# Four feed-forwards split into an up stage and a down stage, the down stage computed with seven block products

## The chip, the cores and the metric

The kernel runs on one core of one Trainium2 chip, in float32 throughout. The metric is device time in microseconds (us), the median over several executions. Engines are named as the profile names them: PE (TensorE, matmul), PEld (its weight load, which overlaps PE), DVE (VectorE), ACT (ScalarE), POOL (GpSimd) and SP (SyncE, which here issues the transfers of the weights).

## The reference, cut to what matters

A first block (modulated norm, hybrid mixer, mixture of experts) is followed by two layers of a second block. Each of these layers runs a feed-forward, a mixer, a cross attention and a feed-forward, so there are four feed-forwards. The sequence has 256 tokens, the model width is 1024, and the hidden width `D_FF` is 2816.

```python
def swiglu_ffn(h, w_in, w_out):
    gate, up = jnp.split(h @ w_in, 2, axis=-1)
    return (jax.nn.silu(gate) * up) @ w_out

for l in range(DEPTH_2):
    x = x + FFN_RES_WEIGHT * swiglu_ffn(rms_norm(x, ffn1_norm_g[l]), ffn1_w_in[l], ffn1_w_out[l])
    ...   # mixer: x + concat(rwkv, moba) @ w_mix_out
    ...   # x + memory_cross_attention(...)
    x = x + FFN_RES_WEIGHT * swiglu_ffn(rms_norm(x, ffn2_norm_g[l]), ffn2_w_in[l], ffn2_w_out[l])
return rms_norm(x, final_norm_g)
```

## The kernel before, in words

**Tiling.** The hidden width is cut into 11 groups `g` of 256 columns (`NGRP`, `FB`). The tokens are two tiles of 128. A matmul takes a stationary tile of 128x128 and a moving tile of up to 512 columns; one call of `nc.tensor.matmul` in float32 is two MATMUL instructions in the trace, each with its own LDWEIGHTS.

**Up-projection of a group** (`up`, PE rows of L2029). Gate and linear columns of one group are a product of (2 halves of K) by (2 halves of tokens) by (gate, linear). Group 0 is done plainly (`up_first`, L2007, 16 products of 128x512). Groups 1 to 10 use the form of Strassen's scheme with seven products P1 to P7, each over four tiles of K with 256 moving columns: 28 matmuls, 56 instructions. It needs sums of the tokens (`Sx`, four, made once for a feed-forward at L2725 to L2730) and sums of the weights (`Tw`, four per group at 128x1024, L2746, L2752, L2756, L2762; two buffers, by `g % 2`). The products go through three PSUM banks, 0 to 2. ACT copies P1 and P5 to SBUF (L2500), DVE adds up the four results (L2771) in `hidden`, ACT takes the silu of the gate (L2503), DVE multiplies gate and linear into `hh` (L2793).

**Turning.** PE transposes `hh` (four tiles, L2015) into bank 3, ACT copies it to `fh` (128x512, two buffers by `g % 2`).

**Down-projection of a group** (`down`, PE rows of L2064). Two tiles of K, two token tiles and two halves of 512 output columns are 8 matmuls of 128x512, 16 instructions. They accumulate over all 11 groups in four banks, 4 to 7, one per token tile and half. The turning of the next group is put in the middle of it.

**Order.** PE runs up(1), down(0), up(2), down(1), then a loop of four turns with up(3), down(2), up(4), down(3), and at last down(10). DVE and ACT run loops of the same kind, and SP issues the pieces of weights in that order: two transfers of 1 MB for an up piece, one of 1 MB for a down piece, in a ring of four slots of 2 MB (`SLOTS`, `ring`). A slot is loaded again once PE has finished with what was in it (semaphores `hid_up` and `hid_down`). The pieces of the mixer and the cross attention follow in the same ring.

**End of a feed-forward.** When the four banks of the down-projection are complete, DVE scales and adds them into `x` (L2824, four instructions of 128x512: two after the first half of the columns, which releases `x_first`, two after the second, which releases `x_ready`). PE then transposes `x` for what follows (L302, `raw_transposes`): banks 0 and 1 wait for `x_first`, banks 2 and 3 for `x_ready`. After the last feed-forward comes the final norm (ACT row sums, POOL, DVE L3099) and the store.

**Beside it.** In the first feed-forward of each layer POOL multiplies the memory by its gain (`gm`, L1959), once `xT` is complete.

## Time and profile before

| what | us |
|---|---|
| median of 3 runs | 2463.85 (2461.95 to 2465.54) |
| the profiled execution, its own time | 2462.07 |
| its span (first to last instruction) | 2460.3 |
| PE busy | 2360.7 (96% of the span) |
| PE, down-projections of the four feed-forwards (L2064) | 315.3 |
| PE, up-projections of groups 1 to 10 (L2029, all five groups of rows) | 214.4 + 144.7 + 75.6 + 75.6 = 510.3 and one smaller |
| DVE busy | 880.2 (36%) |
| DMA, mean | 203 GB/s |

The four feed-forwards stand at about 857 to 1073, 1438 to 1653, 1655 to 1870 and 2233 to 2448 us of the span. The granted TensorE clock has a mean of 0.983 over the span. Busy times of PE are unions of modelled spans: the mean of one instruction (592 ns) is longer than the distance from one start to the next, since matmuls are pipelined, so costs are read from starts.

### The profile page before, as it was taken

How to read it: one execution, taken by the hardware profiler on the slowest of the kernel's cores; microseconds unless marked ns; L12 is line 12 of the kernel's file. 1: busy time of each engine (PE TensorE's matmuls, PEld its weight loads, DVE VectorE, ACT ScalarE, POOL GpSimd, SP SyncE). 2: the span in 40 equal slices, each digit the busy share in tenths (PEclk: the TensorE clock that was granted, in tenths of full speed). 3: DMA queues.
4: the chain of work that ended last, by engine and by line, in shares of the span. 5: the costliest groups of instructions: out<-in, count | busy, mean ns of one | idle time of the engine just before them, and what ended most of it. 6: DMA issues, size and time to landing. Idle time of an engine off the chain costs nothing. (4 is left out here: it accounts for less than half of the span.)

```text
span 2460.3 us, 29787 instructions
## 1 busy us (share of the span) xinstructions
PE 2360.7 (96%) x12188; PEld 1587.7 (65%) x12188; DVE 880.2 (36%) x1620; ACT 424.2 (17%) x832; POOL 47.1 (2%) x75
## 2 busy tenths in 40 slices
PE   7999979999999899999999999999999999999998
PEld 4778744444444377778666757767777867676775
DVE  2888221111111344421542134444442154213443
ACT  1123121111111111111312211111111121221111
POOL 1000000000000000000000000000000000000000
PEclk9999979999999999999999999999999999999999
DMA  9565639999999844452431254454545243124442
GB/s 397 221 257 226 258 102 344 422 422 422 422 422 422 324 138 156 151 194 80 154 121 41 97 163 154 153 171 137 172 135 212 68 147 121 67 71 162 154 163 76
DMA packets 176139, 499.48 MB, mean 203 GB/s; under 512 B 7193, under 2 KB 99625, under 8 KB 146097
## 3 DMA queue, kind: packets, MB, share of 16 engines
q1 hardware_dynamic: 172224, 481.23, 52.3%
q0 software_dynamic: 3680, 16.43, 2.3%
q8 instruction: 68, 1.11, 0.2%
q10 hardware_dynamic: 144, 0.52, 0.1%
q14 instruction: 23, 0.18, 0.0%
HBM read 491.34 MB, written 6.82 MB: 202 GB/s over the span
## 5 line engine op out<-in xcount | busy, mean ns | idle before, releaser
L2064 PE MATMUL bank<-ring,fh 128*128 128x512 f32 x704 | 315.3, 592 | 0.0
L2064 PEld LDWEIGHTS bank<-ring,fh 128*128 128x128 f32 x704 | 130.6, 190 | 132.2 <-issue 130.1
L2029 PE MATMUL bank<-Tw,Sx 128*128 128x256 f32 x960 | 214.4, 379 | 0.0
L2029 PEld LDWEIGHTS bank<-Tw,Sx 128*128 128x128 f32 x960 | 182.1, 190 | 24.6
L2098 PE MATMUL bank<-xT,ring 128*128 128x256 f32 x704 | 152.6, 379 | 0.0
L844 PE MATMUL bank<-xT,ring 128*128 128x256 f32 x640 | 143.7, 384 | 2.8 <-ACT xT L279 2.8
L2098 PEld LDWEIGHTS bank<-xT,ring 128*128 128x128 f32 x704 | 133.4, 190 | 18.0
L2029 PE MATMUL bank<-ring,xT 128*128 128x256 f32 x640 | 144.7, 379 | 0.0
L2029 PEld LDWEIGHTS bank<-ring,xT 128*128 128x128 f32 x640 | 121.6, 190 | 33.6 <-issue 19.1
L2771 DVE TENSOR_TENSOR whole<-bank,part 128x256 f32<-128x256 f32 x120 | 51.0, 425 | 255.6 <-PE bank L2029 255.6
L844 PEld LDWEIGHTS bank<-xT,ring 128*128 128x128 f32 x640 | 122.8, 193 | 21.9 <-ACT xT L279 2.9
L1379 PE MATMUL bank<-ring,xg 128*64 128x512 f32 x512 | 114.3, 594 | 7.1 <-DMA ring<-in_w 7.1
L1416 PE MATMUL bank<-ring,hTg 128*64 128x512 f32 x512 | 113.4, 595 | 0.0
L1379 PE MATMUL bank<-more,xg 128*64 128x512 f32 x512 | 112.6, 592 | 0.0
L2500 ACT ACTIVATE part<-bank 128x256 f32<-128x256 f32 x80 | 30.7, 384 | 346.5 <-PE bank L2029 346.5
L1379 PEld LDWEIGHTS bank<-ring,xg 128*64 128x64 f32 x512 | 36.2, 137 | 82.5 <-issue 68.0
L1696 DVE TENSOR_TENSOR sg<-sg,bank 128x512 f32<-128x512 f32 x16 | 11.0, 688 | 214.0 <-PE bank L1379 214.0
L1416 PEld LDWEIGHTS bank<-ring,hTg 128*64 128x64 f32 x512 | 35.3, 137 | 76.1 <-issue 76.1
L1379 PEld LDWEIGHTS bank<-more,xg 128*64 128x64 f32 x512 | 36.7, 137 | 73.3 <-issue 73.3
L1363 PEld LDWEIGHTS bank<-hot,xs 128*128 128x128 f32 x544 | 64.9, 199 | 17.2 <-issue 13.0
L2029 PE MATMUL bank<-ring,Sx 128*128 128x256 f32 x320 | 75.6, 379 | 0.0
L2029 PE MATMUL bank<-Tw,xT 128*128 128x256 f32 x320 | 75.6, 379 | 0.0
(458 smaller groups left out, 3063.9 us busy)
## 6 DMA issues: line engine op xcount, KB each, us to landing
ring<-in_w SPq DMA_DIRECT2D x128, 1024.0 KB, 18.6
ring<-in_ffn_w_in SPq DMA_DIRECT2D x88, 1024.0 KB, 7.5
ring<-in_first_pieces SPq DMA_DIRECT2D x33, 2048.0 KB, 12.3
more<-in_w SPq DMA_DIRECT2D x64, 1024.0 KB, 19.8
ring<-in_ffn_w_out SPq DMA_DIRECT2D x44, 1024.0 KB, 4.9
ring<-in_w_mix_in SPq DMA_DIRECT2D x12, 2048.0 KB, 9.3
ring<-in_xattn_w_kv SPq DMA_DIRECT2D x8, 2048.0 KB, 11.9
ring<-in_w_mix_out SPq DMA_DIRECT2D x4, 2048.0 KB, 9.7
```

Source lines behind the costliest of these rows:

```text
L844: last = nc.tensor.matmul(b[:, c * SEQ:(c + 1) * SEQ], w[:, k, m * P:(m + 1) * P], xT[:, k, :], start=(k == 0), stop=(k == KD - 1))
L1363: last = nc.tensor.matmul(bank[half][:, k * P:(k + 1) * P], xs[:, t, f:f + P], hot[:, t, :], start=(t == 0), stop=(t == NT - 1))
L1379: last = nc.tensor.matmul(bank[2 + m][e * CAP:(e + 1) * CAP, :], xg[:, 4 * half + k, e * CAP:(e + 1) * CAP], up_rows(4 * m + 2 * half + e) ...
L1416: last = nc.tensor.matmul(bank[half][e * CAP:(e + 1) * CAP, :], hTg[:, c * P + e * CAP:c * P + (e + 1) * CAP], down_rows(8 + 2 * (c // 2) ...
L1696: nc.vector.tensor_tensor(sg[:, 1, :], sg[:, 0, :], bank[3][:, :], ALU.mult).then_inc(h_ready, 1)
L2029: last = nc.tensor.matmul(bank[b][:, 0:SEQ], lhs(k), rhs(k), start=(k == 0), stop=(k == 3))
L2064: last = nc.tensor.matmul(bank[4 + 2 * half + t][:, :], fh[:, g % 2, c * SEQ + t * P:c * SEQ + (t + 1) * P], w[:, c, half * 512:(half + 1) ...
L2098: last = nc.tensor.matmul(b[:, c * SEQ:(c + 1) * SEQ], w[:, k, col:col + P], xT[:, k, :], start=(k == 0), stop=(k == KD - 1))
L2500: nc.scalar.activation(dst, src, ACT.Copy).then_inc(ffn_copied, 1)
L2771: return nc.vector.tensor_tensor(dst, a_, b_, ALU.add)
```

## The change

All up-projections of a feed-forward run first, groups 0 to 10, and the gated rows of all groups stay in SBUF, turned (`fh` has eleven buffers in place of two). Then come the down-projections. In them the two K tiles of a group, the two token tiles and the two halves of the output columns form a two by two by two block product, done as seven matmuls of 128x512 per group. They accumulate over the groups in seven PSUM banks (`BANK_OF`), and the results are combined once at the end. For this DVE makes, per group, four sums of the gated rows (128x128: `Sd0` for group 0, else in `Sx`, four buffers) and four sums of the down weights (128x512, `Td`, four buffers laid over `Tw`).

The up-projections use seven banks in place of three, so most waits between products are gone from `up`, and DVE spreads the four weight sums of the next group between its other work. The loops of PE, DVE, ACT and SP over the groups are written out. Down weights come as six pieces of up to 2 MB (two groups each) in place of eleven of 1 MB; the numbering of the pieces in the ring changes with it. At the end, ACT copies P1 and P5 of the down stage, and DVE needs eleven instructions of 128x512 in place of four: four sums, and seven scaled additions into `x`.

```diff
         ffn = ExitStack()
-        fh = sb("fh", [2, 512], ffn)
+        fh = sb("fh", [NGRP, 512], ffn)
         hh = sb("hh", [NT, SEQ], ffn)
         fs = sb("fs", [NT, SEQ], ffn)
+        Sd0 = sb("Sd0", [4, P], ffn)
+        sb("behind_cross", [1040], ffn)
+
+        Tw = sb("Tw", [2, 4, 4, SEQ], ffn)
+        Td = [Tw[:, 1 - b // 2].rearrange("p a k n -> p (a k n)")[:, (b % 2) * 2048:(b % 2 + 1) * 2048].rearrange(
+            "p (a n) -> p a n", a=4) for b in range(4)]
         gf2_row = sb("gf2_row", [D], ffn)
-
-
-        part = sb("part", [5, SEQ], ffn)
+        sb("behind_gm", [1056], ffn)
+
+        Sx = sb("Sx", [4, 4, P], ffn)
+        part = sb("part", [4, SEQ], ffn)
...
-
-        J_SKIPPED = (29, 34, 41)
-        assert PER_LAYER % SLOTS == 0
+        FB, N_DOWN = NGRP, (NGRP + 1) // 2
+
+
+        J_FFN1, J_MIX, J_KV, J_MIXOUT, J_XQ, J_XO, J_FFN2 = 0, 17, 24, 28, 30, 32, 34
+        PER_LAYER = 52
+
+        J_SKIPPED = (51,)
...
                     else:
-                        read(l, j0 + p - SLOTS)
-                    ffn_piece(l, name, p // 2, p % 2, slot_of(j0 + p))
-
-                def up_piece(g, count):
-                    sp.wait_ge(hid_up, count)
+                        read(l, j - SLOTS)
+                    if q < FB:
+                        dst = slot_w(s, KD, 512)
+                        sp.dma_start(dst[:, :, 0:256], up[:, :, q * 256:(q + 1) * 256]).then_inc(w_full[s], 16)
+                        sp.dma_start(dst[:, :, 256:512],
+                                     up[:, :, D_FF + q * 256:D_FF + (q + 1) * 256]).then_inc(w_full[s], 16)
+                    else:
+                        r = 512 * (q - FB)
+                        k = min(4, (D_FF - r) // P)
+                        load(s, a[name + "_w_out_2"][l][r:r + k * P, :].rearrange("(k p) n -> p k n", p=P), k, D)
...
+                def turned(g):
+                    pe.wait_ge(hid_h, per_piece(f, 1, g, 1))
+                    if g:
+                        pe.wait_ge(ffn_copied, copied(f, "h", g - 1))
                     for c in range(2):
...
-                        if stop and half == 0:
-                            last.then_inc(ffn_out, 1)
-                    last.then_inc(hid_down, 1)
+                    if g > 1:
+                        pe.wait_ge(ffn_copied, copied(f, "P5", g - 1))
+                    product("P1", lambda k: xT[:, k, first], lambda k: w[:, k, gate]).then_inc(ffn_prod, 1)
+                    pe.wait_ge(hid_g, sums(f, "up_weights", g))
+                    product("P2", lambda k: xT[:, 4 + k, first], lambda k: w[:, 4 + k, gate]).then_inc(ffn_prod, 1)
+                    turned(g - 1)
+                    product("P6", S(2), T(2)).then_inc(ffn_prod, 1)
+                    product("P5", S(1), T(1)).then_inc(ffn_prod, 1)
+                    product("P7", S(3), T(3)).then_inc(ffn_prod, 1)
+                    product("P3", S(4), lambda k: w[:, 4 + k, linear]).then_inc(ffn_prod, 1)
+                    product("P4", lambda k: xT[:, 4 + k, second], T(4)).then_inc(hid_up, 1)
+
+                def down(name, g):
+                    s = slot_of(j0 + FB + g // 2)
+                    w = slot_w(s, 4, D)
+                    half, other = slice(0, 512), slice(512, D)
+
+                    def rows(c, t):
+                        return fh[:, g, c * SEQ + t * P:c * SEQ + (t + 1) * P]
+
+                    def S(n_):
+                        return Sd0[:, n_ - 1, :] if g == 0 else Sx[:, (g - 1) % 4, n_ - 1, :]
+
+                    def T(n_):
+                        return Td[g % 4][:, n_ - 1, :]
+
+                    c = 2 * (g % 2)
+                    lhs, rhs = {"P1": (rows(0, 0), w[:, c, half]), "P2": (rows(1, 0), w[:, c + 1, half]),
+                                "P3": (S(4), w[:, c + 1, other]), "P4": (rows(1, 1), T(4)), "P5": (S(1), T(1)),
+                                "P6": (S(2), T(2)), "P7": (S(3), T(3))}[name]
+                    return nc.tensor.matmul(bank[BANK_OF[name]][:, :], lhs, rhs, start=(g == 0), stop=(g == FB - 1))
...
                 up_first()
-                up(1)
-                down(0, start=True)
-                up(2)
-                down(1)
-                with pe.Fori(0, 4) as i:
-                    for g in (3, 4):
-                        up(g, i)
-                        down(g - 1, i)
-                down(10, stop=True)
+                for g in range(1, FB):
+                    up(g)
+                pe.wait_ge(ffn_copied, copied(f, "P5", FB - 1))
+                for g in range(FB - 2):
+                    if g % 2 == 0:
+                        wait_piece2(pe, j0 + FB + g // 2, l)
+                    pe.wait_ge(hid_g, sums(f, "down_weights", g))
+                    for name in ("P1", "P2", "P6", "P5"):
+                        down(name, g)
+                    if g == 0:
+                        turned(FB - 1)
+                    for name in ("P7", "P3", "P4"):
+                        last = down(name, g)
+                    if g % 2:
+                        last.then_inc(hid_down, 1)
+
+                wait_piece2(pe, j0 + FB + (FB - 2) // 2, l)
+                wait_piece2(pe, j0 + FB + (FB - 1) // 2, l)
+                pe.wait_ge(ffn_copied, copied(f, "h", FB - 1))
+                for name in ("P1", "P6", "P5", "P7", "P2", "P4", "P3"):
+                    if name == "P6":
+                        pe.wait_ge(hid_g, sums(f, "down_weights", FB - 1))
+                    first_last = down(name, FB - 2)
+                    last = down(name, FB - 1)
+                    if name == "P3":
+                        first_last.then_inc(hid_down, 1)
+                        last.then_inc(hid_down, 1)
+                    else:
+                        last.then_inc(ffn_prod, 1)
 
             def project(l, m):
...
+                def combine_down(g):
+                    s = wait_piece2(dve, j0 + FB + g // 2, l)
+                    w = slot_w(s, 4, D)
+                    c = 2 * (g % 2)
+                    w11, w12, w21, w22 = (w[:, c + b, h_ * 512:(h_ + 1) * 512] for b in range(2) for h_ in range(2))
+                    dve.wait_ge(ffn_copied, copied(f, "h", g))
+                    if g >= 4:
+                        dve.wait_ge(hid_down, f * N_DOWN + (DOWN_MOE + (g - 4) // 2 + 1))
+                    h11, h21, h12, h22 = (fh[:, g, b * P:(b + 1) * P] for b in range(4))
+                    Sd, T = Sd0 if g == 0 else Sx[:, (g - 1) % 4], Td[g % 4]
+
+                    def minus(dst, a_, b_):
+                        st(nc.vector.tensor_tensor(dst, a_, b_, ALU.subtract))
+
+                    st(nc.vector.tensor_tensor(Sd[:, 0, :], h21, h22, ALU.add))
+                    minus(T[:, 0, :], w12, w11)
+                    minus(Sd[:, 2, :], h11, h21)
+                    minus(T[:, 2, :], w22, w12)
                     st.sync()
-                    st(nc.vector.tensor_tensor(T[:, 1], w22, T[:, 0], ALU.subtract))
-
-                def combine_third(g):
-                    w11, w12, w21, w22 = blocks_of(g)
-                    st(nc.vector.tensor_tensor(Tw[:, g % 2, 2], w22, w12, ALU.subtract))
-
-                def combine_fourth(g):
-                    w11, w12, w21, w22 = blocks_of(g)
-                    T = Tw[:, g % 2]
+                    minus(Sd[:, 1, :], Sd[:, 0, :], h11)
+                    minus(T[:, 1, :], w22, T[:, 0, :])
                     st.sync()
-                    nc.vector.tensor_tensor(T[:, 3], w21, T[:, 1], ALU.subtract).then_inc(hid_g, 1)
-
-
...
+                def hidden(g):
+                    if g < FB - 1:
+                        combine(1, g + 1)
+                    dve.wait_ge(ffn_prod, prod(f, "P2", g))
+                    dve.wait_ge(ffn_copied, copied(f, "P1", g))
+                    add(whole[:, 0, :], ps["P2"], P1).then_inc(hid_g, 1)
+                    if g < FB - 1:
+                        combine(2, g + 1)
+                    dve.wait_ge(ffn_prod, prod(f, "P6", g))
+                    add(U2, ps["P6"], P1).then_inc(hid_g, 1)
+                    if g < FB - 1:
+                        combine(3, g + 1)
+                    dve.wait_ge(ffn_copied, copied(f, "P5", g))
+                    dve.wait_ge(hid_g, sums(f, "P1+P6", g))
+                    st(add(P1, P5, U2))
+                    if g < FB - 1:
+                        combine(4, g + 1)
+                    else:
+                        combine_down(0)
+                    dve.wait_ge(ffn_prod, prod(f, "P7", g))
+                    st(add(U3, ps["P7"], U2))
...
+                E1, E5 = (flat(part[:, 2 * n_:2 * n_ + 2, :]) for n_ in range(2))
+                V2, V3 = (flat(whole[:, 2 * n_:2 * n_ + 2, :]) for n_ in range(2))
+                V4, V5 = flat(hh[:, :, :]), flat(fs[:, :, :])
+                full = {name: bank[b][:, :] for name, b in BANK_OF.items()}
+
+                def to_x(t, half, src):
+                    cs = slice(half * 512, (half + 1) * 512)
+                    return nc.vector.scalar_tensor_tensor(out=x[:, t, cs], in0=src, scalar=rstd[:, t:t + 1],
+                                                          in1=x[:, t, cs], op0=ALU.mult, op1=ALU.add)
+
                 dve.wait_ge(rstd_ready, e + 1)
-                for half in range(2):
-                    if half == 0:
-                        dve.wait_ge(ffn_out, f + 1)
-                    else:
-                        dve.wait_ge(hid_down, f * FB + (DOWN_MOE + FB))
-                    cs = slice(half * 512, (half + 1) * 512)
-                    for t in range(NT):
-                        last = nc.vector.scalar_tensor_tensor(out=x[:, t, cs], in0=bank[4 + 2 * half + t][:, :],
-                                                              scalar=rstd[:, t:t + 1], in1=x[:, t, cs],
-                                                              op0=ALU.mult, op1=ALU.add)
-                    if half == 0:
-                        last.then_inc(x_first, 1)
-                last.then_inc(x_ready, 1)
+                dve.wait_ge(ffn_copied, copied(f, "P1"))
+                st(to_x(0, 0, E1))
+                dve.wait_ge(ffn_prod, prod(f, "P6"))
+                st(add(V2, full["P6"], E1))
+                st.sync()
+                dve.wait_ge(ffn_copied, copied(f, "P5"))
+                st(add(V4, E5, V2))
+                dve.wait_ge(ffn_prod, prod(f, "P7"))
+                st(add(V3, full["P7"], V2))
+                st.sync()
+                st(to_x(0, 1, V4))
+                st(add(V5, E5, V3))
+                dve.wait_ge(ffn_prod, prod(f, "P2"))
+                st(to_x(0, 0, full["P2"]))
+                st(to_x(1, 0, V3))
+                st.sync()
+                dve.wait_ge(ffn_prod, prod(f, "P4"))
+                to_x(1, 0, full["P4"]).then_inc(x_first, 1)
+                st(to_x(1, 1, V5))
+                st.sync()
+                dve.wait_ge(hid_down, f * N_DOWN + (DOWN_MOE + N_DOWN))
+                to_x(0, 1, full["P3"]).then_inc(x_ready, 1)
                 dve.wait_ge(x_ready, e)
 
```

**PE.** What it runs for one group before, straight from group 2: up(2), then down(1) with the turning in it.

```order
L2029 MATMUL bank<-ring,xT 128x256 x8
L2029 MATMUL bank<-Tw,Sx 128x256 x12
L2029 MATMUL bank<-ring,Sx 128x256 x4
L2029 MATMUL bank<-Tw,xT 128x256 x4
L2064 MATMUL bank<-ring,fh 128x512 x4
L2015 MATMUL bank<-K,hh 128x128 x4
L2064 MATMUL bank<-ring,fh 128x512 x4
```

The same engine in the changed kernel, from the end of up(10) to the first products of the second down group; L2023 is the up product, L2063 the down product, L2011 the turning.

```order
L2023 MATMUL bank<-Tw,xT 128x256 x4
L2063 MATMUL bank<-ring,fh 128x512 x2
L2063 MATMUL bank<-Tw,Sd 128x512 x2
L2011 MATMUL bank<-K,hh 128x128 x4
L2063 MATMUL bank<-Tw,Sd 128x512
L2063 MATMUL bank<-ring,Sd 128x512
L2063 MATMUL bank<-Tw,fh 128x512
L2063 MATMUL bank<-ring,fh 128x512 x2
L2063 MATMUL bank<-Tw,Sx 128x512 x3
```

The 8 down products of a group are 7 now, stand behind all up-projections, and read sums made by DVE.

**DVE.** In the last up group (10) before: the sums of the products (L2771), the gating (L2793), and the end of the feed-forward (L2824).

```order
L2771 TENSOR_TENSOR whole<-bank,part 128x256
L2771 TENSOR_TENSOR part<-bank,part 128x256
L2771 TENSOR_TENSOR part<-part 128x256
L2771 TENSOR_TENSOR part<-bank,part 128x256
L2771 TENSOR_TENSOR whole<-part 128x256
L2771 TENSOR_TENSOR whole<-bank,part 128x256 x2
L2793 SCALAR_TENSOR_TENSOR hh<-fs,whole 128x512
L2824 SCALAR_TENSOR_TENSOR x<-bank,rstd,x 128x512 x4
```

The changed kernel in the same group; L2782, L2784 and L2794 are the sums for the first down group, L2802 the sums of products.

```order
L2802 TENSOR_TENSOR part<-part 128x256
L2784 TENSOR_TENSOR Sd<-fh 128x128
L2782 TENSOR_TENSOR Tw<-ring 128x512
L2782 TENSOR_TENSOR Sd<-fh 128x128
L2782 TENSOR_TENSOR Tw<-ring 128x512
L2782 TENSOR_TENSOR Sd<-Sd,fh 128x128
L2782 TENSOR_TENSOR Tw<-ring,Tw 128x512
L2782 TENSOR_TENSOR Sd<-fh,Sd 128x128
L2794 TENSOR_TENSOR Tw<-ring,Tw 128x512
L2802 TENSOR_TENSOR part<-bank,part 128x256
L2802 TENSOR_TENSOR whole<-part 128x256
L2802 TENSOR_TENSOR whole<-bank,part 128x256 x2
```

Eight instructions for the down stage now stand between the third and the fourth sum of the products; eight more per group follow behind the gating.

**DVE, the end.** The changed kernel from its last weight sum on (L2855 is the scaled addition into `x`), where the kernel before has the four rows of L2824.

```order
L2794 TENSOR_TENSOR Tw<-ring,Tw 128x512
L2855 SCALAR_TENSOR_TENSOR x<-part,rstd,x 128x512
L2802 TENSOR_TENSOR whole<-bank,part 128x512
L2802 TENSOR_TENSOR hh<-part,whole 128x512
L2802 TENSOR_TENSOR whole<-bank,whole 128x512
L2855 SCALAR_TENSOR_TENSOR x<-hh,rstd,x 128x512
L2802 TENSOR_TENSOR fs<-part,whole 128x512
L2855 SCALAR_TENSOR_TENSOR x<-bank,rstd,x 128x512
L2855 SCALAR_TENSOR_TENSOR x<-whole,rstd,x 128x512
L2855 SCALAR_TENSOR_TENSOR x<-bank,rstd,x 128x512
L2855 SCALAR_TENSOR_TENSOR x<-fs,rstd,x 128x512
L2855 SCALAR_TENSOR_TENSOR x<-bank,rstd,x 128x512
```

Of these eleven only the last waits for the last product; x_first is released two rows earlier.

## Rows read from the trace of the kernel before

**Rows 1.** The page: PE's share of the span; the group of the down products
```profile
PE 2360.7 (96%) x12188; PEld 1587.7 (65%) x12188; DVE 880.2 (36%) x1620; ACT 424.2 (17%) x832; POOL 47.1 (2%) x75
L2064 PE MATMUL bank<-ring,fh 128*128 128x512 f32 x704 | 315.3, 592 | 0.0
```

**Rows 2.** Timeline of PE, one group: start us, length us, what [idle before]
```profile
892.02 3.62 PE L2029 MATMUL bank<-ring,xT 128*128 128x256 f32 x16
895.48 5.34 PE L2029 MATMUL bank<-Tw,Sx 128*128 128x256 f32 x24
...
904.11 3.60 PE L2064 MATMUL bank<-ring,fh 128*128 128x512 f32 x8
907.54 0.60 PE L2015 MATMUL bank<-K,hh 128*128 128x128 f32 x4
...
911.42 3.62 PE L2029 MATMUL bank<-ring,xT 128*128 128x256 f32 x16
```

**Rows 3.** Windows: length, busy PE, PEld, DVE, ACT, POOL, clock, DMA share, GB/s
```profile
857.30:1073.42 216.12, 216.12 (x813) 150.61 (x813) 92.14 (x130) 26.56 (x58) 4.85 (x3) 0.99 0.47 155
892.02:911.41 19.39, 19.39 (x77) 14.07 (x76) 8.30 (x12) 2.27 (x5) 0.00 (x0) 1.00 0.51 163
840.00:860.00 20.00, 10.10 (x28) 5.98 (x29) 15.04 (x23) 6.41 (x13) 2.08 (x4) 0.74 0.61 204
```

**Rows 4.** Timeline of PE at three other places
```profile
840.60 3.67 PE L1400 MATMUL bank<-ye,whotT 128*128 128x512 f32 x8 [0.89 <-DVE ye L1701]
852.88 1.97 PE L302 MATMUL bank<-K,x 128*128 128x128 f32 x8 [8.61 <-DVE x L1636]
...
1083.37 69.23 PE L2098 MATMUL bank<-xT,ring 128*128 128x256 f32 x320
```

**Rows 5.** Groups of DVE by shape: count, busy us, mean ns, idle before
```profile
L2746 DVE TENSOR_TENSOR Tw<-ring 128x1024 f32<-128x1024 f32 x40 | 52.0, 1299 | 6.0 <-DMA ring<-in_ffn_w_in 5.8
L2824 DVE SCALAR_TENSOR_TENSOR x<-bank,rstd,x 128x512 f32<-128x512 f32 x16 | 11.3, 746 | 44.0 <-PE bank L2064 44.0
L1668 DVE TENSOR_TENSOR whot<-hot,comb 128x128 f32<-128x128 f32 x34 | 8.2, 281 | 0.0
L2725 DVE TENSOR_TENSOR Sx<-xT 128x512 f32<-128x512 f32 x4 | 2.8, 692 | 0.4
```

**Rows 6.** Timeline of DVE in the group of Rows 2
```profile
899.55 0.42 DVE L2771 TENSOR_TENSOR part<-part 128x256 f32<-128x256 f32 x1 [1.72 <-ACT part L2500]
...
904.31 0.43 DVE L2771 TENSOR_TENSOR whole<-bank,part 128x256 f32<-128x256 f32 x1 [0.17 <-PE bank L2029]
905.38 0.69 DVE L2793 SCALAR_TENSOR_TENSOR hh<-fs,whole 128x512 f32<-128x512 f32 x1 [0.65 <-ACT fs L2503]
```

**Rows 7.** Timeline of PE at the end of the first feed-forward
```profile
1073.42 1.04 PE L302 MATMUL bank<-K,x 128*128 128x128 f32 x8
1075.09 1.09 PE L302 MATMUL bank<-K,x 128*128 128x128 f32 x8 [0.63 <-DVE x L2824]
```

**Rows 8.** Timeline of DVE at the same place
```profile
1073.62 1.41 DVE L2824 SCALAR_TENSOR_TENSOR x<-bank,rstd,x 128x512 f32<-128x512 f32 x2 [1.95 <-PE bank L2064]
```

**Rows 9.** Timeline of POOL in the first feed-forward
```profile
861.11 3.63 POOL L1959 TENSOR_TENSOR gm<-memT,lc 128x2048 f32<-128x2048 f32 x1
```

**Rows 10.** Timeline of DVE there, and at two later places
```profile
861.31 4.51 DVE L2746 TENSOR_TENSOR Tw<-ring 128x1024 f32<-128x1024 f32 x1
...
1444.49 1.23 DVE L2746 TENSOR_TENSOR Tw<-ring 128x1024 f32<-128x1024 f32 x1 [2.81 <-DMA ring<-in_ffn_w_in]
...
1659.28 1.23 DVE L2746 TENSOR_TENSOR Tw<-ring 128x1024 f32<-128x1024 f32 x1
```

**Rows 11.** Timeline of SP's queue before the second feed-forward
```profile
1436.56 0.58 SPq L1859 DMA_DIRECT2D ring<-in_ffn_w_in  x1
```

**Rows 12.** Waits: for whom, us in total, times, longest
```profile
PE bank L2284 <- issue: 5.7, 3, 2.2
PE bank L302 <- DVE x L2824: 1.9, 3, 0.6
```

More of the change, by code:

```diff
@@ L1903, in before_layer @@
+            def before_layer(l, p):
+                if l:
+                    read(l - 1, PER_LAYER - SLOTS + p)
+                elif p < 2:
+                    sp.wait_ge(hid_up, UP_MOE - 1 + p)
+                    sp.sem_inc(sp_passed, 1)
+                else:
+                    sp.wait_ge(hid_down, DOWN_MOE - 3 + p)
                     sp.sem_inc(sp_passed, 1)
@@ new lines, in second_gate @@
+                def second_gate(g):
+                    act.wait_ge(hid_g, sums(f, "gate2", g))
+                    silu(1, whole[:, 3, :])
+                act.wait_ge(ffn_prod, prod(f, "first"))
+                silu(0, bank[6][:, 0:SEQ])
+                act.wait_ge(hid_up, UP_MOE + per_piece(f, 1, 0, 1))
+                silu(1, bank[7][:, 0:SEQ])
+                for g in range(1, FB):
+                    if g > 1:
+                        second_gate(g - 1)
+                    act.wait_ge(ffn_prod, prod(f, "P1", g))
+                    copy(part[:, 0, :], bank[BANK_OF["P1"]][:, 0:SEQ])
+                    turned(g - 1)
+                    act.wait_ge(hid_g, sums(f, "gate1", g))
+                    silu(0, whole[:, 0, :])
+                    act.wait_ge(ffn_prod, prod(f, "P5", g))
+                    copy(part[:, 1, :], bank[BANK_OF["P5"]][:, 0:SEQ])
@@ L2532, in take_spread @@
+                second_gate(FB - 1)
+                turned(FB - 1)
+                for n_, name in enumerate(("P1", "P5")):
+                    act.wait_ge(ffn_prod, prod(f, name))
+                    copy(flat(part[:, 2 * n_:2 * n_ + 2, :]), bank[BANK_OF[name]][:, :])
             def take_spread(l, where):
```

270 lines of the change are left out of this document (91 added, 179 removed).

## The prediction, made before the changed kernel had run

> **What bounds the kernel now.** I read the page first: PE is busy for 96% of the span, and the down products are its largest group, 704 instructions with 315.3 us [rows 1]. Then the windows: the first feed-forward, 216.1 us long, has PE busy for all of it, and a window over one group has 19.39 us of PE in 19.39, against 8.30 of DVE, 2.27 of ACT and nothing of POOL, at full clock [rows 3]. Last the timeline of that group: no row of PE has an idle time before it, and the next group begins exactly when the down products end [rows 2]. So inside a feed-forward PE's instruction stream is the time, and everything else lies beside it. What is taken from PE comes off the end one for one, until something else is late.
>
> **Prices.** The mean of 592 ns in [rows 1] is no price, since matmuls overlap. From start to start 8 down instructions take 907.54 - 904.11 = 3.43 us, 0.429 each. The rest of the down group, 911.42 - 907.54 = 3.88, is again 3.43 and 0.45 for the four transposes. The 56 up instructions take 904.11 - 892.02 = 12.09, 0.216 each or 1.73 for a product of eight [rows 2]. Together 19.39, the window of [rows 3].
>
> **Removed.** Eight down matmuls per group become seven: two instructions less per group, 11 groups, 4 feed-forwards, 88 instructions by 0.429 = 37.7 us, all on PE's path. Up products, first products and transposes keep number and shape, so their move costs nothing of itself.
>
> A down product of the new kind goes into another bank each time, and accumulates there over eleven groups. The nearest row is L1400, four products accumulating into four banks in turn: 3.67 us for its 8 instructions, where the 8 of L2064 that change bank every second product show 3.60 [rows 4, 2]. The 0.07 follows an idle time. I take no difference; at worst 0.07 / 8 by 616 instructions = 5.4 us.
>
> **Loops written out.** The group in [rows 2] is group 2, which stands outside the loops, and the 320 instructions of L2098 at 1083.37 are straight code too: 69.23 us, 0.216 each, without a gap [rows 4]. PE has waited for nothing visible ("issue") in L2284, 5.7 us in 3 places, products of 64 columns [rows 12]. Feed-forward instructions are long, so I price this at 0, with 2 us either way where later code shifts.
>
> **DVE in the up stage.** Per group it has four weight sums of 1.2 us, seven sums of 0.43 and one gating of 0.69 [rows 5, 6]: some 8.5 us, now in 12.5 us of PE (12.09 + 0.45) in place of 19.4. I laid it out from the start of P1: products end at 1.73, 3.46, then the turning to 3.91, then 5.64, 7.37, 9.10, 10.83 and 12.55. Each piece of 1.2 us falls between two products, and the weights of the next group are complete more than 4 us before PE asks for them. The old rows wait, gating, turned, all have time: the gating ends 1.07 + 0.69 us after the last sum begins [rows 6], and PE turns it 3.46 us into the next group. Cost 0.
>
> **The seam between the stages.** This is the new wait. In group 10 DVE's third sum starts 7.53 us after P1's start [rows 2, 6], now 0.45 later, and ends at 8.40. Then come the eight sums for down group 0: four of 128x128 at 0.281 and four of 128x512 at 0.692, 3.89 us [rows 5], to 12.29, just before PE is through with P4. The four sums left in the group (4 by 0.43) end at 14.01 instead of some 13.2, the gating at 13.58 + 1.07 + 0.69 = 15.34, and the sums for down group 1 at 19.23. PE reaches group 1 at 12.54 + 14 by 0.429 + 0.45 = 18.99. So PE waits 0.24 us; all seven products of the group are queued behind the wait, and DVE has everything else for them behind it. The other end is no wait: two neighbouring instructions of 0.746 take 1.41 together [rows 5, 8], 0.08 less than their sum, and some ten such joints lie in this stretch. If the 128x128 sums cost what a 256-wide one does (0.43), each block of eight is 0.6 longer, and the wait 1.4 us. For four feed-forwards: 0 to 5.8, I take 0.5, near the end that the joints favour.
>
> After it DVE needs 3.89 us for a group against PE's 14 by 0.429 = 6.0 and runs ahead, up to the four buffers; the last one starts two groups early. Cost 0; without that cover each us over 6.0 would cost 40 us.
>
> **The end of a feed-forward.** Before, two scalings (1.41 us, from 0.20 after the last product) release banks 2 and 3, and PE, whose first eight transposes last 1.04, waits 0.63 [rows 7, 8]; in total 1.9 for three feed-forwards [rows 12]. Now only one instruction of 0.746 stands behind the last product. It ends at 0.95, when the transposes are just out. For DVE to be free then, its eleven instructions must fit behind the products, 1.72 us for each pair of groups (4 by 0.429): counted back from the last product's end, P7 is complete at -5.15, three instructions bring it to -2.9, two for P2 to -1.5, P4 from -1.5 to -0.75, one more to -0.05, then the last at 0.20. It fits. The wait of 0.63 goes, 1.9 us in all, and at the very end 1.41 - 0.75 = 0.7. Were DVE late by the whole of one instruction, these 2.6 us would be a loss of about 0.4.
>
> **Transfers.** The up pieces have slots three groups ahead now. Late is one piece: the second up piece of layer 1, whose slot is free only with the ninth product group, 0.9 us before the feed-forward's end. A piece takes 1444.49 - 1436.56 = 7.9 us until DVE can use it [rows 10, 11], so it is there 7.0 after the end; DVE asks at 1659.28, some 6 us after the end at about 1653 [rows 10]. Its sums take 4 by 1.23 and 3.3 more where POOL's `gm` stands beside one of them (4.51 for 1.23 in [rows 10], POOL's 3.63 in [rows 9]), to 15.2; PE asks after 2.0 of transposes, 32 by 0.429 and one product, 17.4. Cost 0. If the two pieces issued right behind it took equal shares, it would come up to three times as late, 23.7 us, and PE would wait up to 13.6, once.
>
> The Trainium skill bears on that row: "SBUF — State Buffer", section "Who interferes with whom", says that a two-input VectorE instruction reading SBUF and a GpSimd instruction exclude each other for a whole instruction. By that rule the new sums would be held whenever POOL works. The trace agrees on the 4.51 us, but POOL is idle in the group's window [rows 3], so the rule adds nothing to the sum.
>
> **The sum.** 37.7 + 1.9 + 0.7 - 0.5 = 39.8 us. The profiled execution took 2462.07 us (span 2460.3); it becomes 2422.3. The median of the runs before, 2463.85, is 1.8 above it; against that I predict 2424.0.
>
> **The rivals.**
> *New waits eat part of it.* The late piece (up to 13.6, once), the seam (up to 5.8) and bank changes (up to 5.4) come in part: about 10 us lost, 2434. For it: the seam has no margin. Against it: DVE's joints, and the margin of 2.2 us at the piece. 9 in 100.
> *The seventh is bought back.* Each product gets dearer by a seventh (0.061 us an instruction), and the kernel stands at 2462. [rows 4] speaks against it. 3 in 100.
> *DVE becomes the bound of the down stage (slower).* If its eight sums took more than 7.0 us per group, 0.87 each instead of a mean 0.49, 40 groups by 1.0 us would use up the gain. At twice the durations, 7.8 us, it is 40 by 1.8 = 72 us more, less 39.8: 2496. For it: one sum of 1.23 did take 4.51 [rows 10]. Against: that has POOL beside it, which is idle later, and the sums in up groups hold 1.23 beside PE and DMA. 3 in 100.
> *The clock.* After 8.61 us of idle PE the window's clock is 0.74, and 8 transposes take 1.97 us where they take 1.04 at full clock [rows 3, 4, 7]: that is 1.2 in place of 2.4 GHz. Were the down stage run so, 616 by 0.429 = 264 us come on top, 2688; a seventh of it would use up the gain. It takes waits of that length, and I found 0.24. 2 in 100.
>
> Beside the clock stands a rule of the Trainium skill that speaks against this change: "TensorE: Matmul & The Clock Gate", section "A second HAM failure mode: psum-queue depth-cycling", has a kernel whose matmuls cycle through the banks, pause a little between groups and so fall back to the slow clock again and again. By it the time would go the way of the clock rival; the rows of this case show products going through banks at full clock without pauses, and it keeps the 2 in 100 given.
>
> **How the numbers follow.** The forecast has 83 in 100, with its own range of 2421 to 2429: 0 to 5.8 at the seam, 2 us either way for shifted code, and the spread of the runs of before (2461.95 to 2465.54). Rivals of 9, 3, 3 and 2 make up the rest. The whole range reaches a little into the first rival, 2420.5 to 2431. About 0.2%, 5 us, is what a measurement can tell from no change. Faster by more than that: the forecast, the first rival and a little of the second, 0.93; within it 0.02; slower 0.05.
>
> **What would show it.** 616 instructions of the down product with the same 592 ns and 0.429 from start to start; a down group of 6.0 us; feed-forwards of about 206.7 us, 9.4 less each; PE's wait for DVE at the seam below 0.5 us; no wait of L302 for `x` after a feed-forward; the eight sums in 3.5 to 3.9 us. The forecast is wrong if PE waits in every down group for DVE's sums, if a ring piece holds up(1) of layer 1, if the starts of down products lie more than 0.43 apart, or if the clock drops below 1.00 in a down stage.

## The result, and the profile after

The changed kernel takes 2418.6 us (median of 4 runs, 2418.5 to 2421.1) against 2464.4 for the kernel before, measured again beside it (4 runs, 2462.0 to 2465.5). The ratio is 0.9816, with a 95% interval of 0.9803 to 0.9828. That is 45.8 us faster. The forecast was 2424.0 us with a range of 2420.5 to 2431.0: the direction is right, and the time came out 1.9 us below the range.

The profiled execution took 2418.74 us (span 2417.0). The page's line of engines and the down products by shape, where [rows 1] had one group of 704:

```profile
PE 2323.6 (96%) x12100; PEld 1573.5 (65%) x12100; DVE 1048.7 (43%) x2000; ACT 428.6 (18%) x840; POOL 46.1 (2%) x75
L2063 PE MATMUL bank<-Tw,Sx 128*128 128x512 f32 x240 | 108.9, 592 | 0.0
L2063 PE MATMUL bank<-ring,fh 128*128 128x512 f32 x176 | 82.7, 593 | 0.0
L2063 PE MATMUL bank<-Tw,fh 128*128 128x512 f32 x88 | 44.3, 592 | 0.0
L2063 PE MATMUL bank<-ring,Sx 128*128 128x512 f32 x80 | 40.2, 592 | 0.0
L2063 PE MATMUL bank<-Tw,Sd 128*128 128x512 f32 x24 | 11.6, 593 | 0.0
```

With the 8 instructions that have `ring` and `Sd` as inputs these are 616, as counted, each of the same 592 ns as in [rows 1], and PE was never idle before one (the last number).

Windows over the first feed-forward, one down group, and the second feed-forward, in the columns of [rows 3]:

```profile
855.36:1065.79 210.43, 209.74 (x806) 149.83 (x807) 138.64 (x232) 29.15 (x63) 5.83 (x4) 0.99 0.45 150
1005.71:1011.72 6.01, 6.01 (x16) 2.67 (x15) 5.80 (x15) 0.00 (x0) 0.00 (x0) 1.00 0.13 51
1422.13:1629.53 207.40, 207.40 (x808) 148.00 (x807) 133.55 (x229) 30.43 (x64) 3.74 (x6) 1.00 0.45 150
```

A down group takes 6.01 us, all of it PE at full clock, with 5.80 us of DVE beside it while DVE works ahead. The second feed-forward has PE busy for all of its 207.40 us. From transposes to transposes the same one took 216.84 before: 9.44 less.

PE's timeline at the seam between the stages, and DVE's beside it:

```profile
999.26 1.88 PE L2063 MATMUL bank<-ring,fh 128*128 128x512 f32 x4
1000.98 1.88 PE L2063 MATMUL bank<-Tw,Sd 128*128 128x512 f32 x4
1002.69 0.60 PE L2011 MATMUL bank<-K,hh 128*128 128x128 f32 x4
...
1005.71 1.88 PE L2063 MATMUL bank<-ring,fh 128*128 128x512 f32 x4
1007.42 2.74 PE L2063 MATMUL bank<-Tw,Sx 128*128 128x512 f32 x6
...
1011.72 1.88 PE L2063 MATMUL bank<-ring,fh 128*128 128x512 f32 x4
```

```profile
1000.87 0.69 DVE L2833 SCALAR_TENSOR_TENSOR hh<-fs,whole 128x512 f32<-128x512 f32 x1 [0.57 <-ACT fs L2516]
1001.48 0.28 DVE L2784 TENSOR_TENSOR Sx<-fh 128x128 f32<-128x128 f32 x1
...
1004.46 0.69 DVE L2794 TENSOR_TENSOR Tw<-ring,Tw 128x512 f32<-128x512 f32 x1
1005.07 0.28 DVE L2784 TENSOR_TENSOR Sx<-fh 128x128 f32<-128x128 f32 x1
```

The eight sums for group 1 run from 1001.48 to 1005.15, and the next block starts at 1005.07. One block is 3.6 us long, where I had 3.89. PE starts group 1 at 1005.71 without a wait.

The end of the first feed-forward, on PE and on DVE, where [rows 7, 8] had two halves with 0.63 us between them:

```profile
1065.79 2.17 PE L302 MATMUL bank<-K,x 128*128 128x128 f32 x16
```

```profile
1065.01 0.74 DVE L2855 SCALAR_TENSOR_TENSOR x<-fs,rstd,x 128x512 f32<-128x512 f32 x1
1066.06 0.75 DVE L2855 SCALAR_TENSOR_TENSOR x<-bank,rstd,x 128x512 f32<-128x512 f32 x1 [0.31 <-PE bank L2063]
```

**Where the 43.3 us between the two profiled executions went.** I cut both traces at the starts of the transposes L302 and compared the pieces.

| piece | before | after | difference |
|---|---|---|---|
| up to the first feed-forward's products | 857.30 | 859.77 | +2.47 |
| 1st feed-forward, from these products | 216.12 | 206.02 | -10.10 |
| mixer of layer 0, with the transposes ahead | 283.72 | 277.60 | -6.12 |
| cross attention, both layers | 157.47 | 157.48 | 0 |
| 2nd feed-forward | 216.84 | 207.40 | -9.44 |
| 3rd feed-forward | 217.56 | 207.53 | -10.03 |
| mixer of layer 1 | 282.41 | 282.25 | -0.16 |
| 4th feed-forward | 216.84 | 207.40 | -9.44 |
| after the last product | 12.04 | 11.55 | -0.49 |

The terms of the forecast come to 4 by 9.44, 3 by 0.63 and 0.49: 40.1 us. The forecast's sum was 39.8. (Two of the waits of 0.63 stand at the head of the mixer rows, the third at the head of the third feed-forward.) Against 43.3 the terms lack 3.2 us. The mixers gave 5.0 more than their two waits, although the change does not touch their code, and the first feed-forward 0.7 more than 9.44; the stretch ahead of it took 2.5 back.

**The mixers.** In each there is a stage of some 60 us made of 64-column products (L2284 before, L2297 after). From PE's last wait for `pmT` ahead of it to its wait for `lw` behind it (ACT writes both), it takes, in windows of before and then of after:

```profile
1259.86:1324.03 64.17, 59.98 (x1364) 56.23 (x1364) 28.79 (x43) 11.06 (x20) 0.53 (x1) 0.97 0.24 85
2055.12:2119.57 64.45, 59.86 (x1364) 56.16 (x1364) 28.77 (x43) 11.06 (x20) 0.54 (x1) 0.97 0.24 84
```

```profile
1250.02:1310.29 60.27, 58.27 (x1365) 54.74 (x1365) 28.75 (x43) 11.06 (x20) 0.53 (x1) 1.00 0.16 55
2024.26:2086.20 61.94, 59.63 (x1365) 56.08 (x1365) 28.77 (x43) 11.05 (x20) 0.54 (x1) 0.97 0.17 54
```

The instructions are the same; the time is 3.90 and 2.51 us shorter, and the DMA share (the column before the last) is 0.16 in place of 0.24. PE's timeline of before, in the first of these windows, has two gaps in which it waited for nothing that the trace shows ("issue"):

```profile
1269.87 0.85 PE L2284 MATMUL bank<-xT,cw 64*64 64x64 f32 x22 [1.76 <-issue]
...
1276.07 1.22 PE L2211 MATMUL bank<-pT 64*128 64x128 f32 x7 [1.73 <-issue]
1277.22 1.97 PE L2284 MATMUL bank<-xT,cw 64*64 64x64 f32 x32
...
1280.13 1.10 PE L2284 MATMUL bank<-xT,cw 64*64 64x64 f32 x32
```

The row at 1277.22 also shows the clock: 32 such products take 1.97 us there and 1.10 three us later. Over 1274 to 1279 the granted clock was 0.70. After, there is one gap:

```profile
1262.07 1.38 PE L2297 MATMUL bank<-pT,xs 64*64 64x64 f32 x40 [1.15 <-issue]
```

What differs is when SP issues the two 2 MB pieces of the cross attention's query weights. Its queue, before and then after:

```profile
1259.05 0.99 SPq L1851 DMA_DIRECT2D ring<-in_xattn_w_q  x2
```

```profile
1224.53 25.05 SPq L1865 DMA_DIRECT2D ring<-in_xattn_w_q  x2
```

Before, both go out within 0.99 us at the start of the stage. After, they are 25 us apart, and only the second falls into the stage. The cause is the new numbering in the ring. A piece waits until the piece four places ahead of it is used up. Before, the first query piece (37) waited for the last key and value piece (33). The second (38) looked back at a skipped number (34) and through it at the first of those pieces (30), so it had nothing left to wait for and went out right behind the first. Now the pieces 30 and 31 wait for the third and the fourth key and value piece (26 and 27).

### The profile page after: what moved, and what is told of

It is laid out like the page before. It is cut to its first block and busy times, and to the rows that moved or that the text cites. A ratio compares the mean times of both kernels' runs of the same rounds, so it can differ in the third digit from the quotient of the medians.

```text
span 2417.0 us, 28952 instructions
## 1 busy us (share of the span) xinstructions
PE 2323.6 (96%) x12100; PEld 1573.5 (65%) x12100; DVE 1048.7 (43%) x2000; ACT 428.6 (18%) x840; POOL 46.1 (2%) x75
## 5 line engine op out<-in xcount | busy, mean ns | idle before, releaser
L2023 PE MATMUL bank<-Tw,Sx 128*128 128x256 f32 x960 | 213.9, 380 | 0.0
L2023 PEld LDWEIGHTS bank<-Tw,Sx 128*128 128x128 f32 x960 | 179.6, 190 | 22.4
L2023 PE MATMUL bank<-ring,xT 128*128 128x256 f32 x640 | 144.7, 379 | 0.0
L847 PEld LDWEIGHTS bank<-xT,ring 128*128 128x128 f32 x640 | 122.9, 193 | 21.6 <-ACT xT L279 2.9
L2023 PEld LDWEIGHTS bank<-ring,xT 128*128 128x128 f32 x640 | 121.9, 190 | 18.0 <-issue 1.9
L2063 PE MATMUL bank<-Tw,Sx 128*128 128x512 f32 x240 | 108.9, 592 | 0.0
L2802 DVE TENSOR_TENSOR whole<-bank,part 128x256 f32<-128x256 f32 (+1 forms) x124 | 53.7, 433 | 100.9 <-PE bank L2023 99.7
L2513 ACT ACTIVATE part<-bank 128x256 f32<-128x256 f32 (+1 forms) x88 | 35.4, 403 | 346.8 <-PE bank L2063 218.4
L2063 PEld LDWEIGHTS bank<-Tw,Sx 128*128 128x128 f32 x240 | 45.7, 190 | 57.3 <-issue 57.3
L2063 PE MATMUL bank<-ring,fh 128*128 128x512 f32 x176 | 82.7, 593 | 0.0
L2516 ACT ACTIVATE fs<-whole,rstd 128x256 f32<-128x256 f32 x80 | 40.3, 503 | 214.4 <-DVE whole L2802 214.4
L1704 DVE COPY ye<-bank 128x512 f32<-128x512 f32 x16 | 11.1, 692 | 150.3 <-PE bank L1419 150.3
```

Of the source, the lines that this page charges most:

```text
L847: last = nc.tensor.matmul(b[:, c * SEQ:(c + 1) * SEQ], w[:, k, m * P:(m + 1) * P], xT[:, k, :], start=(k == 0), stop=(k == KD - 1))
L2023: last = nc.tensor.matmul(bank[BANK_OF[name]][:, 0:SEQ], lhs(k), rhs(k), start=(k == 0), stop=(k == 3))
L2063: return nc.tensor.matmul(bank[BANK_OF[name]][:, :], lhs, rhs, start=(g == 0), stop=(g == FB - 1))
L2513: nc.scalar.activation(dst, src, ACT.Copy).then_inc(ffn_copied, 1)
L2516: nc.scalar.activation(fs[:, t, :], src, ACT.Silu, scale=rstd[:, t:t + 1]).then_inc(hid_silu, 1)
L2802: return nc.vector.tensor_tensor(dst, a_, b_, ALU.add)
```

## The experiments

The theory: the missing 5 to 6 us come from these transfers, which hold up PE while it runs short instructions; the feed-forwards give what the forecast says. The rivals are that the gain lies in the written-out loops or the new order of the feed-forwards; or the mixers' difference is chance. The first four kernels ran beside 15 runs of the kernel before (median 2463.7), the last three beside 12 (2464.9).

**The changed kernel without those transfers in the stage.** SP holds both query pieces until the mixer's scan is over.

```diff
+                    if j == J_XQ:
+                        sp.wait_ge(gn_xc, l * 2 + 2)
+                        sp.sem_inc(sp_passed, 1)
```

> The changed kernel, with both query-weight pieces of the cross attention (2 MB each) held back until the group norm of the mixer has begun, so that no weights move while PE runs the inverse stage (L2297, products of 64 columns). Transfer theory: waits of PE for instructions there (1.15 us in layer 0, 1.61 in layer 1) and the low clock behind them come from the weight transfers; both go, the stretch from the last attention product to L2390 shrinks from 60.3 and 61.9 us to about 57.5, and the kernel to 2411 to 2413 us. Rival, the stage depends on where its code lies or on chance: it stays at 60 to 62 us and the kernel at 2417 to 2421.

Measured: 2413.5 us (2412.6 to 2414.8, 5 runs), ratio 0.9794 (0.9780 to 0.9807). It is the fastest of all kernels here, and 0.5 us above the range expected. The pieces go out at 1315.27, behind the stage. The first stage, in a window:

```profile
1252.49:1311.02 58.53, 57.83 (x1364) 54.52 (x1365) 28.67 (x43) 11.06 (x20) 0.53 (x1) 1.00 0.06 21
```

The second is 58.54, so both are 1.0 longer than the 57.5 expected. The two stages together are 5.1 us shorter than in the changed kernel (117.1 against 122.2), and so is the median of the runs (2413.5 against 2418.6). No gap without a releaser is left in them.

**The same edit in the kernel before.**

> The kernel before, with the same hold on both query-weight pieces (there they are issued together, at the start of the inverse stage). Transfer theory: the stretch shrinks from 64.2 and 64.5 us to about 57.5, the kernel from 2464 to about 2451. Rival (code position or chance): no change, 2462 to 2466.

Measured: 2454.6 us (2453.0 to 2456.1), ratio 0.9960 (0.9946 to 0.9973), stages of 58.53 and 58.78 us and again no such gaps. Some 9 us go without any edit to a feed-forward, where 13 were expected. So the cost belongs to the transfers, not to the loops or to the code's new place.

**The changed kernel with the pieces together again**, as before: the first is held until the last key and value piece is used.

```diff
+                    if j == J_XQ:
+                        sp.wait_ge(kv_psum, l * 8 + 8)
+                        sp.sem_inc(sp_passed, 1)
```

> The changed kernel, with the first query-weight piece held until the last key-value product, so that both pieces are issued together as in the kernel before. Transfer theory: the stretch goes back from 60.3 and 61.9 us to about 64.3, and the kernel is 6 us slower, about 2425: just the part of the gain that the prediction had not seen. Rival (the written-out feed-forward code has moved this stage to a better place): it stays at 60 to 62 us, the kernel at 2419.

Measured: 2423.5 us (2421.8 to 2424.1), ratio 0.9833 (0.9819 to 0.9846). Two gaps are back in each stage (0.27 and 1.97, 0.33 and 2.01 us), and the stages take 62.76 and 61.35. The time is near the forecast, 2424.0, but only in part for the expected reason. The stages were to come back to 64.3 us each, and together they are only 1.9 us longer than in the changed kernel. The two profiled executions are 4.7 us apart (spans 2421.7 and 2417.0). Of the other 2.8 us, 1.0 stands ahead of the first feed-forward, 1.6 in it with its transposes, and 0.3 behind the waits for `bon`, all in code that this edit leaves alone. So this run shows the direction and the gaps, not the size.

**One piece held, in the kernel before**: the edit of the second experiment, for `J_XQ + 1` in place of `J_XQ`.

> The kernel before with only the second of the two pieces of the cross-attention's query weights held back until the mixer's scan is over, the first one issued where it always was. If it is the transfers beside the inverse stage that cost TensorE time, one piece costs about half of what two cost: the stretch from the last wait for a transposed product to the gate's wait, 64.2 and 64.5 us with two pieces and 58.5 and 58.8 with none, comes to 60 to 62 us, with one wait for instructions of 1 to 2 us in each, and the kernel to about 2459 us. If instead it is only that the two pieces run together that matters, the stretch comes to 58.5 to 59.5 and the kernel to 2455 us.

Measured: 2458.3 us (2455.6 to 2460.6), ratio 0.9975 (0.9965 to 0.9985). The stages take 60.31 and 60.32 us, with one gap each, as PE's list of its rows with waits shows:

```profile
PE bank L2287 <- issue: 2.8, 2, 1.5
```

In the kernel before, then, the stage takes 58.5 to 58.8 us with no piece in it, 60.3 with one and 64.2 to 64.5 with two. Over all nine kernels it is 58.5 to 58.8 with none (4 stages), 59.5 to 61.9 with one (10 stages) and 61.4 to 64.5 with two (4 stages). Part of the spread is the clock: the three stages at the upper end, of 61.9, 64.2 and 64.5 us, and the one of 62.8 have a granted clock of 0.97, the others 1.00.

**The new order with eight plain products**: all up-projections first and down-projections after them, but no sums and the old end.

```diff
-                    lhs, rhs = {"P1": (rows(0, 0), w[:, c, half]), "P2": (rows(1, 0), w[:, c + 1, half]),
...
+                        for t in range(NT):
+                            for c in range(2):
+                                last = nc.tensor.matmul(bank[4 + 2 * half + t][:, :],
+                                                        fh[:, g, c * SEQ + t * P:c * SEQ + (t + 1) * P],
+                                                        w[:, 2 * (g % 2) + c, half * 512:(half + 1) * 512],
```

> The changed kernel with its two stages, seven banks in the up stage, ring and transfers, but with the down stage as eight plain products per group in four banks, no sums of rows or weights, and the old end (four scalings). If the seventh product is the gain (88 instructions by 0.429 us and 2.6 us at the ends), it takes 2418.6 + 37.7 + 2.6 = 2459 us. Rival, that the order in two stages with more banks gives something itself: less than 2455. Rival, that DVE's sums cost PE something now: less than 2456 too, with down groups shorter than 6.86 us of PE.

Measured: 2458.0 us (2455.5 to 2465.1, 10 runs), ratio 0.9977 (0.9968 to 0.9986). Its second feed-forward, in a window:

```profile
1435.60:1652.44 216.84, 216.84 (x829) 151.91 (x828) 89.61 (x133) 29.23 (x62) 3.74 (x6) 1.00 0.46 152
```

216.84 us is what the kernel before has to the hundredth: order and written-out loops are worth nothing there. It gains 5.7 us in all. In its trace (span 2457.2 against 2460.3) the two stages with the query pieces are 9.2 us shorter than before, and the part ahead of the first feed-forward and the stretches behind the waits for `bon` are 3.4 and 3.2 us longer. From here to the changed kernel, the seventh product with its sums and its end, it is 39.4 us, against 39.8 in the forecast.

**The sums of the down stage made twice** (all eight, in groups 1 to 10).

```diff
+                    for again in range(1 if g == 0 else 2):
...
+                        st(nc.vector.tensor_tensor(Sd[:, 0, :], h21, h22, ALU.add))
```

> The changed kernel with the VectorE sums of the down stage (groups 1 on) written twice, the second time over the same values, so that a group's sums take about 2 x 3.6 = 7.2 us of VectorE against TensorE's 6.0 us a group. If VectorE can bound the down stage once its share passes TensorE's (the rival of the prediction), each of the 4 feed-forwards grows by about 1.2 to 1.3 us for each of its some 10 groups after the lead that VectorE has from the bank reads is used up: 40 to 55 us in all, 2460 to 2474 us, with TensorE waits for VectorE at the starts of the groups. If the sums are free whatever their length, the time stays at 2418.6 us, within 1.

Measured: 2502.5 us (2499.3 to 2503.2), ratio 1.0147 (1.0130 to 1.0164), slower than the kernel before. PE's waits, and its timeline from the middle of a down stage to the end:

```profile
PE bank L2063 <- DVE Tw L2798: 67.8, 36, 6.5
```

```profile
1022.75 1.98 PE L2063 MATMUL bank<-ring,fh 128*128 128x512 f32 x4 [0.96 <-DVE Tw L2798]
...
1030.15 1.96 PE L2063 MATMUL bank<-ring,fh 128*128 128x512 f32 x4 [1.12 <-DVE Tw L2798]
...
1065.43 1.88 PE L2063 MATMUL bank<-ring,fh 128*128 128x512 f32 x4
1073.85 7.74 PE L2063 MATMUL bank<-Tw,Sx 128*128 128x512 f32 x12 [6.55 <-DVE Tw L2798]
```

The groups of the middle now start 7.3 us apart on average, the length of the doubled sums, 1.3 more than 6.01, as expected. But the kernel lost 84 us, not 40 to 55. The first feed-forward grew by 21.6: 3.2 at the seam, 9.1 over seven groups, and 9.2 at the end, which I had not thought of. The last two groups are woven product by product, so both sets of sums must be there after the first four instructions. PE waits 6.55 us, and the clock over the next 7.6 us is 0.69, which costs 2.4 more. The mechanism is shown; the size that I expected was wrong.

**A smaller dose**: two more sums of 128x512 per group.

```diff
+                    if g:
+                        minus(T[:, 0, :], w12, w11)
+                        minus(T[:, 2, :], w22, w12)
+                        st.sync()
```

> The changed kernel with two more 128x512 sums in each down group, about 1.4 us more, so some 5.0 to 5.1 us of VectorE a group, still under TensorE's 6.0. By the bound as a threshold: nothing per group, and at most the seam of each feed-forward grows by the same 1.1 to 1.4 us where the sums of the first group end late, 4 to 5 us in all at most: 2418.6 to 2423.5 us, and the down groups still start 6.0 us apart. If VectorE's length counted in proportion instead (contention for memory, or waits of each group), each group would grow, by 0.3 us or more each, and the time would pass 2430 us.

Measured: 2419.2 us (2417.9 to 2422.3), ratio 0.9811 (0.9794 to 0.9827), the same as the changed kernel. A block of sums takes 4.92 us, and PE waits only at the seam:

```profile
1007.35 1.98 PE L2063 MATMUL bank<-ring,fh 128*128 128x512 f32 x4 [0.67 <-DVE Tw L2798]
...
1013.46 1.88 PE L2063 MATMUL bank<-ring,fh 128*128 128x512 f32 x4
```

Each of the second and third feed-forwards is 0.93 us longer, and the down groups of the first still start 6.0 to 6.1 us apart. So DVE's length does not count until it passes PE's: 3.6 and 4.9 us cost nothing per group, 7.3 cost all that is over 6.0.

## Why the prediction was right, and where it was wrong

**What bounds the kernel, Prices, Removed: right.** 88 instructions by 0.429 are 37.7 us; four feed-forwards lost 9.44 each, 37.8, beside the ends (the first another 0.7). The kernel with eight products gives the same from the other side.

**Bank changes at 0: right.** Down groups of 7 products into seven banks take 6.01 us, 14 by 0.429. The worst case of 5.4 us did not come.

**DVE in the up stage, the seam, the sums: right, by less than was thought.** PE's waits for the eight sums are 0; the 0.5 us taken for the seam was 0.5 too much. Only PE's weight load shows the wait at all, 1.0 us over four seams. The joints between neighbouring DVE instructions, noted in the prediction, made the block 3.6 us and not 3.89. With 1.3 us more, PE waits 0.67: the seam really had about 0.6 us to spare, where the working had it short by 0.24.

**The end of a feed-forward: right.** The three waits of 0.63 are gone, and no row of L302 waits for `x` after a feed-forward. The last stretch gave 0.49 for 0.7.

**Transfers of the feed-forwards: right.** The late piece's second half was issued at 1629.34, 0.2 us before the feed-forward's end where the prediction had 0.9, and DVE could use it 8.0 us later, where [rows 10, 11] gave 7.9. The equal sharing with the pieces behind it, which would have cost up to 13.6 us, did not occur:

```profile
1637.30 3.40 DVE L2759 TENSOR_TENSOR Tw<-ring 128x1024 f32<-128x1024 f32 x1 [1.83 <-DMA ring<-in_ffn_w_in]
```

```profile
1636.02 3.59 POOL L1954 TENSOR_TENSOR gm<-memT,lc 128x2048 f32<-128x2048 f32 x1
```

PE ran on through its products meanwhile. The DVE sum lasts 3.40 us for a usual 1.23: POOL's `gm` is at work until 1639.61, and the sum is through 1.09 us after that. The Trainium skill, "SBUF — State Buffer", section "Who interferes with whom", has a VectorE instruction with two SBUF inputs contend with a GpSimd instruction that reads SBUF. The trace agrees here, as [rows 9, 10] did.

**"Loops written out", priced at 0 "with 2 us either way where later code shifts": the step that failed.** The prediction saw the 5.7 us of gaps in L2284 [rows 12] and put them down to short instructions and to where the code lies. It passed over a fourth gap of 1.7 us beside them (1276.07, L2211), and never asked what else ran in those stretches. They lie where both query pieces arrive, and the renumbering of the ring, which stood in the diff (`J_SKIPPED`), moved one of the two away. The section on transfers followed the ring inside the feed-forwards alone. The term missing is 5.7 us by the medians of the kernel with eight products, 6.4 by the two stages in the profiled pair: 39.8 and 5.7 are 45.5, against 45.8 measured. So close an agreement is partly luck, since single executions differ by more than 0.3 us outside the terms. The range of the prediction was too narrow at the fast end for the same reason: it allowed for 2 us of this kind.

**Chance in one execution.** Between the wait for `bon` and the wait for `pmT` just before that stage, the same code took 10.20 to 13.31 us in the eighteen stretches of nine traces, by how far the clock fell after that wait: in the kernel before, the 16 products of L2211 right behind it took 2.03 us in a stretch of 11.81, and 1.16 in one of 10.20. In the profiled pair it took 22.0 us before and 23.4 after, in the two layers together; most others had 11.7 to 11.9 a piece. The part ahead of the first feed-forward varies too, by 2.5 us in this pair. So the pair adds up: 40.1 of the terms, 6.4 of the stages and 0.7 in the first feed-forward, less 1.4 and 2.5, are the 43.3 us between the profiles, where the medians are 45.8 apart.

**The clock and the rule of the banks.** The granted clock is 1.00, the level of 2.4 GHz, in the down group above, whose products go round seven banks. The Trainium skill's warning in "TensorE: Matmul & The Clock Gate", section "A second HAM failure mode: psum-queue depth-cycling", is of matmuls that cycle through the banks and idle briefly between their groups. It did not come true here: there are no pauses between these groups. Where I made a pause of 6.55 us, the clock over the following 7.6 us was 0.69, between the levels of 1.2 and 2.4 GHz.

**What stays open.** Why the transfers hold PE up. In the 25 us from 1255 to 1280 of the kernel before, the DMA engines carried this:

```profile
q1 hardware_dynamic: 2080, 4.19, 48.5%
q0 software_dynamic: 144, 1.05, 10.0%
q8 instruction: 3, 0.05, 0.9%
```

The queue q8 carries instructions (packets, MB, share) through the same engines while the kernel runs. Asked for in windows of 0.1 us, its packets stand in a fixed relation to the gaps: in the seven kernels that have gaps in the stage, each of the 18 gaps ends 2.2 to 2.6 us after one of these packets. In the kernel before, two packets stand at 1267.4 and 1273.5, and PE goes on at 1269.87 and 1276.07. In the changed kernel they stand at 1259.8 and 2034.3, and PE goes on at 1262.07 and 2036.68. Packets come later beside the weights: counted from the start of the first stage, the first two stand at 7.5 and 13.6 us before, and at 4.8 and 8.4 in the same kernel with the pieces held, which has no gap. The gaps themselves need no transfer beside them. These are the windows over both gaps of the changed kernel:

```profile
1260.90:1262.07 1.17, 0.02 (x2) 0.00 (x1) 0.04 (x1) 0.00 (x0) 0.00 (x0) 1.00 0.00 0
2035.07:2036.68 1.61, 0.00 (x1) 0.00 (x0) 0.69 (x1) 0.00 (x0) 0.00 (x0) 1.00 0.00 0
```

The last two columns say that nothing moves; the weights had just arrived. So it is not the weights' traffic of that moment that stops PE. Instructions that came late behind the weights are the reading that fits. It is not proven, since the rows of the transfers do not say for which engine a packet was. That the weights' transfers are the cause is shown by the two kernels that hold both pieces back and the one that holds one; the kernel with the pieces together agrees in direction.

## What to carry to other kernels

Where the matmul engine's instruction stream is the time, a product of a block scheme taken out is worth its full price, as long as the vector engine's sums for a group stay below the matmul time of the group; a seam or woven groups at the end can need more than the mean. When a change renumbers a shared ring, follow every issue of the ring through the whole program, not only those of the stages that are edited. A gap without a releaser in a stage of short matmuls is to be held against the DMA columns of the same window and of the few us before it: large transfers that are not needed soon are better issued behind such a stage.

## What the runs showed of the hardware that was not expected

PE, in 64-column products, stood still for up to 2.3 us during or just after the transfer of one or two 2 MB pieces, which ran at up to 403 GB/s over 5 us. One piece in the stage cost 1.0 to 3.4 us against 58.5 without, two 2.8 to 5.9. Every such gap ended 2.2 to 2.6 us after a packet of the instruction queue. In the feed-forwards, where an instruction lasts 0.216 to 0.429 us from start to start, transfers cost nothing: they ran at 150 GB/s on average, and at 362 over the 5 us from 1490 in the changed kernel, with PE busy throughout. The clock behind a gap differed: over the 5 us after one gap of 1.61 us in the changed kernel it was 0.67, and after one of 2.03 us in the kernel with two more sums it was 1.00. Eight VectorE sums in a row (four of 128x128, four of 128x512) took 3.6 us, 0.3 less than the sum of their lengths.
